# Two-layer encoder trunk on one core: the FFN's up product with the weights stationary and h born transposed

## Chip, cores and metric

One Trainium2 chip, one of its cores, one launch. The time is the device time of the whole program in microseconds (us). A kernel's time is the median of its runs.

## What is computed

`x` is (256 tokens, 1024). Each of two layers does FFN, mixer, FFN, each followed by a residual with a layer norm. The change touches the FFNs alone, which run four times:

```
def swiglu_ffn(x, w_up, w_down):          # w_up (1024, 2*2816), w_down (2816, 1024)
    gate, up = jnp.split(x @ w_up, 2, axis=-1)
    return (jax.nn.silu(gate) * up) @ w_down
x = layer_norm(ALPHA * x + 0.5 * swiglu_ffn(x, ffn1_w_up[l], ffn1_w_down[l]), ln1_g[l], ln1_b[l])
```

The mixer (a state-space branch and a sparse attention branch) stays as it is.

## The kernel before

**Products in three parts.** Every large product is made of fp32r matmuls on operands split in a high and a low part: `split_mm` issues hi·hi, hi·lo and lo·hi into the same PSUM bank (L617, L618, L619). ScalarE makes the high part of a weight slice (`whi`, L366, a copy of `raw`), VectorE the low part (`wlo`, L1009, `raw` minus `whi`). `x` is split in the same way (`xh`, `xl`).

**Weight slices.** SyncE loads slices of 128 x 1024 floats into `raw`, a ring of 4 buffers; `whi` and `wlo` are rings of 8. A slice may be split once TensorE has used the slice 8 places earlier, which the semaphore `pe_used` tells, and `raw` is loaded again when the slice in it is split (`split_done`).

**Up phase of an FFN.** The 2816 features go in 11 chunks of 256. A chunk has 4 weight slices; each holds two groups of 128 input rows, and for each 256 gate and 256 up columns. `up_pass` runs over a token tile t of 128 tokens: 8 x 3 matmuls, tokens stationary (128x128), 512 weight columns moving. A pass fills one bank: gate in one half, up in the other, tokens on partitions. Two passes make a chunk. Then ScalarE takes silu of the gate half (L387), VectorE multiplies it by the up half and 0.5 (L1035, `h`). `h_transpose` (L643) turns `h` of a chunk on TensorE, four transposes of 128x128, one chunk later; ScalarE copies the turned bank to `hh` (L378) and VectorE makes `hl` (L1025), because the down product needs features on partitions. The first two chunks are interleaved (`first_chunks`): pass 0 of both, then pass 1 of both, as the second token tile of `x` is ready later.

**Order.** Each engine has its own list, written out by hand. In chunk c, VectorE does: `h` of token tile 0, the four `wlo` of the slices of chunk c+2, `h` of tile 1, `hl` of chunk c-1. ScalarE has silu, four `whi`, silu, `hh`. The four `whi` wait for pass 1 of chunk c, which gives the slices free one by one.

**Down phase.** 22 slices, 12 matmuls of 512 columns each. In the first two FFNs ("first" and "second" in time) GpSimd (POOL) meanwhile prepares tables for the mixer of a layer (`prepare`): a long chain of elementwise operations on SBUF, begun early in the up phase. After the first down slice TensorE waits for its semaphore `bbar_ready` and turns its result (L723).

Of the kernel before, what the change touches and what calls it, by code (L numbers as in the profile page):

```python
# [68 lines left out]
OUT0 = BRS0 + BRANCH_Q  # L69
PEEL = 3  # L70
# [18 lines left out]
def build(nc, A, out):  # L89
# [10 lines left out]
    xh = sb("xh", [P, KT, SEQ], F32R)  # L100
    xl = sb("xl", [P, KT, SEQ], F32R)
# [40 lines left out]
    silu = place("silu", [P, NT, CW])  # L142
    h = place("h", [P, 2, NT, CW])
# [58 lines left out]
    for name in ("hi_done split_done pe_used ident_landed const_landed affine_landed const_ready tok_ready "  # L202
                 "xt_done xh_done x_ready up_done silu_done h_ready ht_done hh_done h_split acc_done "
# [9 lines left out]
    ACC = [2, 6]  # L213
    XT = [4, 6]
# [30 lines left out]

    def wait_up(eng, i, f, s, c, t):
# [18 lines left out]
    def xt_view(i):  # L265
        return ps[:, XT[i]:XT[i] + 2, :].rearrange("p b (k n) -> p (b k) n", n=P)
# [11 lines left out]
    with block:  # L278
# [80 lines left out]
        def _(act):  # L359
# [12 lines left out]
            def x_hi(t, i):  # L372
                act.wait_ge(S["xt_done"], 2 * t + i + 1)
                nc.scalar.copy(xh[:, :, tok(i)], xt_view(i)).then_inc(S["xh_done"], 1)  # L374

            def h_hi(f, c, b):
                act.wait_ge(S["ht_done"], steps(f, c) + 1)
                nc.scalar.copy(hh[:, bass.ds(2 * c, 2), :],  # L378
                               ps[:, 4 + b, :].rearrange("p (k n) -> p k n", k=2)).then_inc(S["hh_done"], 1)

            def up_chunk(i, f, s, c, b, first=False):
                for t in range(NT):
                    wait_up(act, i, f, s, c, t)
                    if not first:

                        act.wait_ge(S["h_ready"], 2 * steps(f, c) + t - 1)
                    nc.scalar.activation(silu[:, t, :], ps[:, 2 * b + t, 0:CW], ACT.Silu  # L387
                                         ).then_inc(S["silu_done"], 1)
# [3 lines left out]
                if not first:  # L392
                    h_hi(f, c - 1, 1 - b)
# [31 lines left out]
            def ffn(f, s0, prep):  # L425
                for c in range(PEEL):
                    up_chunk(0, f, s0 + 4 * c, c, c % 2, first=c == 0)
# [4 lines left out]
                    if c == 1 and prep is not None:  # L432
                        prepare_angles(prep)
                with act.Fori(0, LOOP_I) as i:
                    for e in range(2):
                        up_chunk(i, f, s0 + 4 * (PEEL + e), 2 * i + PEEL + e, (PEEL + e) % 2)
                for k in range(HK - RING):
                    splits(s0 + UP_Q + RING + k, 1)
                    if k == 5:
                        h_hi(f, NC_UP - 1, (NC_UP - 1) % 2)  # L440
# [84 lines left out]
            def mixer(l):  # L525
# [57 lines left out]
                def m_hi(t):  # L583
                    act.wait_ge(S["mt_done"], NT * l + t + 1)
                    src = xt_view(1) if t == 0 else ps[:, 0:2, :].rearrange("p b (k n) -> p (b k) n", n=P)
# [28 lines left out]
        def _(pe):  # L614
# [12 lines left out]
            def x_transpose(stage, i):  # L627
# [4 lines left out]
                for k in range(KT):  # L632
                    ins = nc.tensor.transpose(ps[:, XT[i] + k // 4, (k % 4) * P:(k % 4 + 1) * P],  # L633
# [3 lines left out]
            def h_transpose(f, c, b, reused=True):  # L637
                if reused:
                    pe.wait_ge(S["h_split"], steps(f, c) - 1)
                pe.wait_ge(S["h_ready"], 2 * steps(f, c) + 2)  # L640
                for k in range(2):
                    for i in range(NT):
                        ins = nc.tensor.transpose(ps[:, 4 + b, k * SEQ + i * P:k * SEQ + (i + 1) * P],  # L643
                                                  h[:, b, i, k * P:(k + 1) * P], ident[:, :])
                ins.then_inc(S["ht_done"], 1)

            def up_pass(i, f, s, c, b, t, wait_bank=True, between=None):

                if wait_bank:
                    pe.wait_ge(S["h_ready"], 2 * steps(f, c - 2) + t + 1)  # L650
                for q in range(4):
                    if t == 0:
                        wait_split(s + q, i)
                    for kk in range(2):
                        k = 2 * q + kk
                        a, b2 = kk * 512, kk * 512 + 512
                        ins = split_mm(ps[:, 2 * b + t, :], xh[:, k, tok(t)], xl[:, k, tok(t)],
# [8 lines left out]
            def up_chunk(i, f, s, c, b):  # L666
                for t in range(NT):
                    up_pass(i, f, s, c, b, t)

            def first_chunks(f, s, stage, prep):  # L670

                pe.wait_ge(S["x_ready"], 2 * stage + 1)
                up_pass(0, f, s, 0, 0, 0, False)
                up_pass(0, f, s + 4, 1, 1, 0, False, lambda: x_transpose(stage, 1))
                pe.wait_ge(S["x_ready"], 2 * stage + 2)
                up_pass(0, f, s, 0, 0, 1, False)
# [9 lines left out]
                up_pass(0, f, s + 4, 1, 1, 1, False)  # L686
                h_transpose(f, 0, 0, False)
# [9 lines left out]
            def late_pass(f, s, k0, n, ah, al, stage):  # L697


                for k in range(k0, n):  # L700
# [3 lines left out]
                    ins = wide_k(s + k, k, 0, ah, al, ACC[0], n - 1)  # L704
                ins.then_inc(S["acc_done"], 1)
                for k in range(k0, n):
                    ins = wide_k(s + k, k, 1, ah, al, ACC[1], n - 1)
# [31 lines left out]
            def ffn(f, stage, s0, following, prep):  # L739
                first_chunks(f, s0, stage, prep)  # L740
                for c in range(2, PEEL):
                    up_chunk(0, f, s0 + 4 * c, c, c % 2)
                    h_transpose(f, c - 1, (c - 1) % 2, False)
                with pe.Fori(0, LOOP_I) as i:
                    for e in range(2):
                        c = 2 * i + PEEL + e
                        up_chunk(i, f, s0 + 4 * (PEEL + e), c, (PEEL + e) % 2)
                        h_transpose(f, c - 1, (PEEL + e - 1) % 2)
                s = s0 + UP_Q
                for k in range(HK - RING):  # L750
# [3 lines left out]
                    for t in range(NT):  # L754
                        ins = wide_k(s + k, k, t, hh, hl, ACC[t], HK - 1)
                    ins.then_inc(S["pe_used"], 1)
                    if k == 5:
                        h_transpose(f, NC_UP - 1, (NC_UP - 1) % 2)
# [140 lines left out]
            def mixer(l):  # L899
# [59 lines left out]
                for k in range(OUT_Q):  # L959
                    wait_split(mix(l, OUT0 + k))  # L960
                    ins = wide_k(mix(l, OUT0 + k), k, 0, xh, xl, ACC[0], OUT_Q - 1)
# [5 lines left out]
                for k in range(OUT_Q):  # L967
                    ins = wide_k(mix(l, OUT0 + k), k, 1, xh, xl, ACC[1], OUT_Q - 1)
# [23 lines left out]
        def _(dve):  # L992
# [24 lines left out]
            def x_lo(stage, i):  # L1017
                dve.wait_ge(S["xh_done"], 2 * stage + i + 1)
                nc.vector.tensor_tensor(xl[:, :, tok(i)], xt_view(i), f32(xh[:, :, tok(i)]), ALU.subtract  # L1019
                                        ).then_inc(S["x_ready"], 1)  # L1020

            def h_lo(f, c, b):
                dve.wait_ge(S["hh_done"], steps(f, c) + 1)
                k = bass.ds(2 * c, 2)
                nc.vector.tensor_tensor(hl[:, k, :], ps[:, 4 + b, :].rearrange("p (k n) -> p k n", k=2),  # L1025
                                        f32(hh[:, k, :]), ALU.subtract).then_inc(S["h_split"], 1)

            def up_chunk(i, f, s, c, b, first=False, early=False):
                for t in range(NT):
                    dve.wait_ge(S["silu_done"], 2 * steps(f, c) + t + 1)  # L1030
                    if not early:

                        dve.wait_ge(S["ht_done"], steps(f, c) - 1)

                    nc.vector.scalar_tensor_tensor(out=h[:, b, t, :], in0=silu[:, t, :], scalar=0.5,  # L1035
                                                   in1=ps[:, 2 * b + t, CW:2 * CW], op0=ALU.mult,
                                                   op1=ALU.mult).then_inc(S["h_ready"], 1)
# [3 lines left out]
                if not first:  # L1041
                    h_lo(f, c - 1, 1 - b)

            def norm(n, s_end, i, aff):

                wait_acc(dve, n, s_end, i)
                for j in range(2):
                    cols = slice(512 * j, 512 * j + 512)
                    ins = nc.vector.scalar_tensor_tensor(out=x[:, i, cols], in0=x[:, i, cols], scalar=ALPHA,  # L1049
                                                         in1=ps[:, ACC[i] + j, :], op0=ALU.mult, op1=ALU.add)  # L1050
# [42 lines left out]
            def ffn(f, s0, prep):  # L1093
                for c in range(PEEL):
                    up_chunk(0, f, s0 + 4 * c, c, c % 2, first=c == 0, early=c < 2)
                    if c == 0 and prep is not None:
                        dve.wait_ge(S["par_t_ready"], 2 * prep + 1)
                        nc.vector.tensor_scalar(small[:, 0, :], par_t[:, 0:NJ], LAM_MAX, None, ALU.min
                                                ).then_inc(S["par_t_ready"], 1)
                with dve.Fori(0, LOOP_I) as i:  # L1100
                    for e in range(2):
                        up_chunk(i, f, s0 + 4 * (PEEL + e), 2 * i + PEEL + e, (PEEL + e) % 2)
# [496 lines left out]
```

## Time and profile before

| | |
|---|---|
| median of 3 runs | 1272.18 us (1271.83 to 1276.61) |
| the profiled execution | 1275.78 us, its span 1274.0 us |
| mean granted TensorE clock | 0.985 |
| busy: PE, VectorE (DVE), ScalarE (ACT), POOL | 1213.6, 781.9, 537.4, 405.2 us |

PE's busy time is modelled and overlapping (a 512-column matmul is shown with 0.39 us but the next starts after less), so how fast TensorE goes is read from start to start. Times in the timeline are us from the span's start.

### The profile page before, as it was taken

To read this page: it belongs to the slowest core of one execution; us is meant where nothing else is said; L and a number is where in the kernel's file an instruction comes from. 1 tells how busy PE (TensorE), PEld (TensorE's weight loads), DVE (VectorE), ACT (ScalarE), POOL (GpSimd) and SP (SyncE) were. 2 spreads that over 40 slices of the span, in tenths; PEclk is the share of its full clock that TensorE was granted. 3 is DMA by queue.
4 is the path that set the end of the run, shared out by engine and by line. 5 is a ranking of instruction groups with operands and counts; after the bars stand their busy time and mean duration, and the time that the engine had idled before them with its cause. 6 is when DMAs were issued, how large, how long until landed. Compare 5 with 4: busy or idle time off the path is not lost.

```text
span 1274.0 us, 17993 instructions
## 1 busy us (share of the span) xinstructions
PE 1213.6 (95%) x5952; PEld 980.3 (77%) x5952; DVE 781.9 (61%) x1278; ACT 537.4 (42%) x753; POOL 405.2 (32%) x599
## 2 busy tenths in 40 slices
PE   6999999989999989999999999989899999999997
PEld 5888777767677878887778888878677778788885
DVE  4657656567666775574376555375586668655543
ACT  5544432424435345443245444243344453544530
POOL 2889891141140068898600000002303300000000
PEclk9999999989999999999999999999899999999999
DMA  8757543542523575565447566445234345657640
GB/s 247 221 176 229 197 167 91 162 145 67 157 80 118 179 220 188 173 224 175 135 134 228 184 214 214 149 133 170 79 104 126 105 156 173 191 179 226 200 165 33
DMA packets 158289, 207.51 MB, mean 163 GB/s; under 512 B 13096, under 2 KB 107624, under 8 KB 158224
## 3 DMA queue, kind: packets, MB, share of 16 engines
q1 hardware_dynamic: 154352, 201.18, 49.5%
q10 hardware_dynamic: 2848, 3.89, 1.2%
q0 software_dynamic: 1024, 1.61, 0.6%
q8 instruction: 37, 0.61, 0.2%
q14 instruction: 28, 0.23, 0.1%
HBM read 205.56 MB, written 1.06 MB: 162 GB/s over the span
## 4 chain that ended last, share of the span: by engine, by line
PE 61%; POOL 23%; DVE 8%; issue 4%; ACT 2%; DMA 1%; POOLq 0%; SPq 0%; ACTq 0%; DVEq 0%
PE ps L617 17%; PE ps L619 16%; PE ps L618 16%; POOL small L1337 7%; POOL b_bar L1337 4%; DVE wlo L1009 3%; POOL tmp L1337 2%; POOL tab_s L1337 2%; POOL tab_c L1337 1%; POOL tab_s L1464 1%; PE ps L789 1%; PE ps L811 1%; PE ps L808 1%; PE ps L790 1%; PE ps L837 1%
## 5 line engine op out<-in xcount | busy, mean ns | idle before, releaser
L1009 DVE TENSOR_TENSOR wlo<-raw,whi 128x1024 fp32r<-128x1024 f32 (+1 forms) x372 | 474.3, 1292 | 241.2 <-ACT whi L366 227.5
L366 ACT CAST whi<-raw 128x1024 fp32r<-128x1024 f32 (+1 forms) x372 | 385.3, 1043 | 328.3 <-PE ps L619 289.3
L617 PE MATMUL ps<-whi,xh 128*128 128x512 f32 x1088 | 440.1, 405 | 12.4 <-DVE xl L1019 6.5
L619 PE MATMUL ps<-whi,xl 128*128 128x512 f32 x1088 | 426.3, 392 | 0.0
L618 PE MATMUL ps<-wlo,xh 128*128 128x512 f32 x1088 | 425.7, 391 | 0.0
L617 PEld LDWEIGHTS ps<-whi,xh 128*128 128x128 f32 x1088 | 207.3, 191 | 61.7 <-DVE xl L1019 7.4
L619 PEld LDWEIGHTS ps<-whi,xl 128*128 128x128 f32 x1088 | 206.8, 190 | 43.9
L618 PEld LDWEIGHTS ps<-wlo,xh 128*128 128x128 f32 x1088 | 207.7, 191 | 37.9
L1361 POOL TENSOR_TENSOR rstd<-var_eps,cst 128x1 f32<-128x1 f32 x12 | 18.2, 1517 | 555.2 <-DVE var_eps L1056 555.2
L617 PE MATMUL ps<-whi,hh 128*128 128x512 f32 x352 | 141.0, 401 | 0.0
L619 PE MATMUL ps<-whi,hl 128*128 128x512 f32 x352 | 138.7, 394 | 0.0
L618 PE MATMUL ps<-wlo,hh 128*128 128x512 f32 x352 | 137.9, 392 | 0.0
L1035 DVE SCALAR_TENSOR_TENSOR h<-silu,ps 128x256 f32<-128x256 f32 x88 | 36.5, 416 | 96.9 <-ACT silu L387 96.9
L387 ACT ACTIVATE silu<-ps 128x256 f32<-128x256 f32 x88 | 33.2, 379 | 139.0 <-PE ps L619 138.3
L1538 POOL TENSOR_TENSOR h_st<-tab_c,g_st 128x256 f32<-128x256 f32 x16 | 18.7, 1166 | 189.2 <-DVE g_st L1141 153.8
L619 PEld LDWEIGHTS ps<-whi,hl 128*128 128x128 f32 x352 | 66.5, 189 | 14.8
L618 PEld LDWEIGHTS ps<-wlo,hh 128*128 128x128 f32 x352 | 66.5, 189 | 13.9
L617 PEld LDWEIGHTS ps<-whi,hh 128*128 128x128 f32 x352 | 66.6, 189 | 13.3
L1337 POOL TENSOR_TENSOR small<-small 128x16 f32<-128x16 f32 x102 | 40.5, 397 | 8.5 <-ACT small L409 0.7
L1049 DVE SCALAR_TENSOR_TENSOR x<-x,ps 128x512 f32<-128x512 f32 x24 | 16.5, 686 | 43.1 <-PE ps L619 42.6
L374 ACT CAST xh<-ps 128x1024 fp32r<-128x1024 f32 x12 | 12.2, 1014 | 45.6 <-PE ps L633 45.6
L1025 DVE TENSOR_TENSOR hl<-ps,hh 128x512 f32 (+1 forms) x44 | 30.0, 683 | 0.0
(178 smaller groups left out, 1223.8 us busy)
## 6 DMA issues: line engine op xcount, KB each, us to landing
raw<-in_ffn_w_up SPq DMA_DIRECT2D x352, 256.0 KB, 4.0
raw<-in_ffn_w_down SPq DMA_DIRECT2D x176, 256.0 KB, 3.0
raw<-in_w_in SPq DMA_DIRECT2D x128, 256.0 KB, 3.2
raw<-in_w_branch SPq DMA_DIRECT2D x32, 256.0 KB, 2.8
raw<-in_w_out SPq DMA_DIRECT2D x32, 256.0 KB, 3.3
bias_g<-bias_rows ACTq DMA_DIRECT2D x16, 192.0 KB, 3.6
raw<-in_w_in SPq DMA_DIRECT2D x16, 148.0 KB, 2.3
affine<-in_ln_g SPq DMA_DIRECT2D x4, 512.0 KB, 5.5
```

Of the source, the lines that this page charges most:

```text
L366: nc.scalar.copy(whi[:, s % RING, 0:w], raw[:, s % RAW, 0:w]).then_inc(S["hi_done"], 1)
L387: nc.scalar.activation(silu[:, t, :], ps[:, 2 * b + t, 0:CW], ACT.Silu).then_inc(S["silu_done"], 1)
L617: nc.tensor.matmul(o, ah, bh, start=start, stop=False)
L618: nc.tensor.matmul(o, ah, bl, start=False, stop=False)
L619: return nc.tensor.matmul(o, al, bh, start=False, stop=stop)
L1009: nc.vector.tensor_tensor(wlo[:, s % RING, 0:w], raw[:, s % RAW, 0:w], f32(whi[:, s % RING, 0:w]), ALU.subtract).then_inc(S["split_done"], 1)
L1025: nc.vector.tensor_tensor(hl[:, k, :], ps[:, 4 + b, :].rearrange("p (k n) -> p k n", k=2), f32(hh[:, k, :]), ALU.subtract).then_inc(S["h_s ...
L1035: nc.vector.scalar_tensor_tensor(out=h[:, b, t, :], in0=silu[:, t, :], scalar=0.5, in1=ps[:, 2 * b + t, CW:2 * CW], op0=ALU.mult, op1=ALU. ...
L1049: ins = nc.vector.scalar_tensor_tensor(out=x[:, i, cols], in0=x[:, i, cols], scalar=ALPHA, in1=ps[:, ACC[i] + j, :], op0=ALU.mult, op1=ALU ...
L1337: ins = nc.gpsimd.tensor_tensor(o, a, b, f)
L1361: nc.gpsimd.tensor_tensor(rstd[:, i, :], var_eps[:, i, :], cst[:, 0:1], ALU.pow).then_inc(S["rstd_ready"], 1)
L1538: nc.gpsimd.tensor_tensor(h_re, co, g_re, ALU.mult)
```

## The change

The first two chunks of an FFN stay as they are (`tok_chunk`, tokens stationary). From chunk 2 on (`up_block`) a 128x128 block of weights is stationary and all 256 tokens move. For the 128 features t of a chunk, gate (g = 0) in bank 2t and up (g = 1) in bank 2t+1: `whi` meets `xh` and `xl` side by side, 512 moving columns, and `wlo` meets `xh`, 256 columns, added onto the first half. The bank then holds two halves that have yet to be added; VectorE does it for both banks with one `tensor_reduce` (`up_sum`). silu and the product run from SBUF to SBUF, `h` has its features on partitions, and its transposes are gone for these chunks. `hh` and `hl` are made from `h` in SBUF.

```diff
-            def up_chunk(i, f, s, c, b):
-                for t in range(NT):
-                    up_pass(i, f, s, c, b, t)
+            def up_block(i, f, s, c, t, after_tokens=False):
+                if after_tokens:
+                    pe.wait_ge(S["h_ready"], 2 * steps(f, t) + NT)
+                else:
+                    pe.wait_ge(S["sum_done"], sums(f, c - 1, t))
+                for g in range(2):
+                    both = ps[:, 2 * t + g, :].rearrange("p (v n) -> p v n", v=2)
+                    for q in range(4):
+                        if t == 0 and g == 0:
+                            wait_split(s + q, i)
+                        for kk in range(2):
+                            k = 2 * q + kk
+                            a = kk * 512 + g * CW + t * P
+                            nc.tensor.matmul(both, w(whi, s + q, a, a + P), xs[:, :, k, :], start=k == 0, stop=False)
+                            ins = nc.tensor.matmul(both[:, 0], w(wlo, s + q, a, a + P), xh[:, k, :], start=False,
+                                                   stop=k == KT - 1)
+                        if t == 1 and g == 1:
+                            ins.then_inc(S["pe_used"], 1)
+                    if after_tokens and t == 0 and g == 0:
+                        h_transpose(f, TOK_CHUNKS - 1)
+                if t == 0:
+                    ins.then_inc(S["up_done"], 1)
...
+            def up_chunk(i, f, s, c, tokens=False):          # VectorE
+                h_lo(f, c - 1, tokens)
+                for t in range(2):
+                    wait_up(dve, i, f, s, c, t)
+                    if not tokens:
+                        dve.wait_ge(S["h_ready"], 2 * steps(f, c - 1) + t + 1)
+                    nc.vector.tensor_reduce(up_sum[:, t, :, :],
+                                            ps[:, 2 * t:2 * t + 2, :].rearrange("p g (v n) -> p g n v", v=2),
+                                            mybir.AxisListType.X, ALU.add).then_inc(S["sum_done"], 1)
                     if t == 0:
+                        dve.wait_ge(S["h_split"], steps(f, c))
+                        for q in range(2):
                             split_lo(i, s + RING + q)
+                    dve.wait_ge(S["silu_done"], 2 * steps(f, c) + t + 1)
+                    nc.vector.scalar_tensor_tensor(out=h[:, t, :], in0=up_sum[:, t, 0, :], scalar=0.5,
+                                                   in1=up_sum[:, t, 1, :], op0=ALU.mult, op1=ALU.mult
+                                                   ).then_inc(S["h_ready"], 1)
+                    if t == 0:
+                        for q in range(2, 4):
+                            split_lo(i, s + RING + q)
...
-                    if k == 5:
-                        h_transpose(f, NC_UP - 1, (NC_UP - 1) % 2)
```

Two places of the order matter below. The first is TensorE at the start of chunk 2. Before, chunk 2 begins right behind the transposes of chunk 0, and those of chunk 1 follow only after all its 48 matmuls. The end of chunk 2 before (names: result <- moving, stationary):

```order
L617 MATMUL ps<-whi,xh 128x512
L618 MATMUL ps<-wlo,xh 128x512
L619 MATMUL ps<-whi,xl 128x512
L643 MATMUL ps<-ident,h 128x128 [waits h_ready]
L643 MATMUL ps<-ident,h 128x128 x3
```

Now, in the first quarter of chunk 2, behind its 16th matmul:

```order
L707 MATMUL ps<-xs,whi 128x512 [waits split_done]
L708 MATMUL ps<-xs,wlo 128x256
L707 MATMUL ps<-xs,whi 128x512
L708 MATMUL ps<-xs,wlo 128x256
L672 MATMUL ps<-ident,up_sum 128x128 [waits h_ready]
L672 MATMUL ps<-ident,up_sum 128x128 x3
L707 MATMUL ps<-xs,whi 128x512
L708 MATMUL ps<-xs,wlo 128x256
```

The transposes of chunk 1, with their wait for `h` of chunk 1, moved from the end of chunk 2 to its first quarter.

The second is VectorE in a chunk of the loop. Before:

```order
L1035 SCALAR_TENSOR_TENSOR h<-silu,ps 128x256 [waits ht_done,silu_done]
L1009 TENSOR_TENSOR wlo<-raw,whi 128x1024 [waits hi_done] x4
L1035 SCALAR_TENSOR_TENSOR h<-silu,ps 128x256 [waits ht_done,silu_done]
L1025 TENSOR_TENSOR hl<-ps,hh 128x512 [waits hh_done]
```

Now (the last chunk ahead of the loop, which has the loop's order):

```order
L1095 TENSOR_REDUCE up_sum<-ps 128x512 [waits up_done]
L1056 TENSOR_TENSOR wlo<-raw,whi 128x1024 [waits hi_done,h_split]
L1056 TENSOR_TENSOR wlo<-raw,whi 128x1024 [waits hi_done]
L1104 SCALAR_TENSOR_TENSOR h<-up_sum 128x256 [waits silu_done]
L1056 TENSOR_TENSOR wlo<-raw,whi 128x1024 [waits hi_done] x2
L1095 TENSOR_REDUCE up_sum<-ps 128x512 [waits pe_used]
L1104 SCALAR_TENSOR_TENSOR h<-up_sum 128x256 [waits silu_done]
```

The second reduction stands behind all four `wlo`, and it is what sets `sum_done` for TensorE's second block of the next chunk. `h` and, in the loop, `hl` read two tiles of SBUF instead of one and PSUM.

## Rows read from the trace of the kernel before

**Rows 1.** The page, part 1: busy us, share of the span, instructions.

```profile
PE 1213.6 (95%) x5952; PEld 980.3 (77%) x5952; DVE 781.9 (61%) x1278; ACT 537.4 (42%) x753; POOL 405.2 (32%) x599
```

**Rows 2.** Timeline of PE, one loop chunk of the third FFN: start, duration, engine, line.

```profile
697.21 0.48 PE L617 MATMUL ps<-whi,xh 128*128 128x512 f32 x1
...
702.78 0.39 PE L617 MATMUL ps<-whi,xh 128*128 128x512 f32 x1
...
708.23 0.60 PE L643 MATMUL ps<-ident,h 128*128 128x128 f32 x4
708.59 0.48 PE L617 MATMUL ps<-whi,xh 128*128 128x512 f32 x1
```

**Rows 3.** Timeline of PE, GLU of the mixer: first of 48 and what follows.

```profile
396.13 0.28 PE L617 MATMUL ps<-xh,whi 128*128 128x256 f32 x1
...
401.87 0.39 PE L617 MATMUL ps<-whi,ya_h 128*128 128x512 f32 x1
```

**Rows 4.** Timeline of PE: start of chunk 2 in FFNs two, three and four.

```profile
471.78 0.48 PE L617 MATMUL ps<-whi,xh 128*128 128x512 f32 x1
...
674.51 0.47 PE L617 MATMUL ps<-whi,xh 128*128 128x512 f32 x1
...
1101.17 0.48 PE L617 MATMUL ps<-whi,xh 128*128 128x512 f32 x1
```

**Rows 5.** Timelines of ACT and DVE: the end of chunk 1, same FFNs.

```profile
475.50 0.41 DVE L1035 SCALAR_TENSOR_TENSOR h<-silu,ps 128x256 f32<-128x256 f32 x1
...
676.93 1.05 ACT L366 CAST whi<-raw 128x1024 fp32r<-128x1024 f32 x1 [0.34 <-DMA raw<-in_ffn_w_up]
...
679.15 0.41 DVE L1035 SCALAR_TENSOR_TENSOR h<-silu,ps 128x256 f32<-128x256 f32 x1
...
1105.53 0.42 DVE L1035 SCALAR_TENSOR_TENSOR h<-silu,ps 128x256 f32<-128x256 f32 x1
```

**Rows 6.** Timelines of ACT and DVE in that loop chunk; four `wlo` back to back.

```profile
703.07 0.39 ACT L387 ACTIVATE silu<-ps 128x256 f32<-128x256 f32 x1 [4.20 <-PE ps L619]
704.34 1.05 ACT L366 CAST whi<-raw 128x1024 fp32r<-128x1024 f32 x1 [0.89 <-PE ps L619]
...
709.66 0.58 ACT L378 CAST hh<-ps 128x512 f32 x1
...
705.43 5.31 DVE L1009 TENSOR_TENSOR wlo<-raw,whi 128x1024 fp32r<-128x1024 f32 x4 [1.53 <-ACT whi L366]
710.66 0.42 DVE L1035 SCALAR_TENSOR_TENSOR h<-silu,ps 128x256 f32<-128x256 f32 x1
710.99 0.69 DVE L1025 TENSOR_TENSOR hl<-ps,hh 128x512 f32 x1
...
647.00 4.62 DVE L1009 TENSOR_TENSOR wlo<-raw,whi 128x1024 fp32r<-128x1024 f32 x4
```

**Rows 7.** Groups of DVE by shape: busy us, mean ns, idle before.

```profile
L1019 DVE TENSOR_TENSOR xl<-ps,xh 128x1024 fp32r<-128x1024 f32 x12 | 14.7, 1223 | 10.3 <-ACT xh L374 10.3
L1053 DVE BATCH_NORM_STATS2 stats<-x 128x6 f32<-128x512 f32 x24 | 16.7, 695 | 0.8
```

**Rows 8.** Timelines of POOL and DVE, late in the first two up phases.

```profile
101.72 1.05 POOL L1337 TENSOR_TENSOR b_bar<-tab_s,small 128x512 f32<-128x512 f32 x1
...
106.10 2.03 POOL L1337 TENSOR_TENSOR b_bar<-tab_s,small 128x512 f32<-128x512 f32 x1
...
103.96 7.48 DVE L1009 TENSOR_TENSOR wlo<-raw,whi 128x1024 fp32r<-128x1024 f32 x4 [1.42 <-ACT whi L366]
...
536.90 8.14 DVE L1009 TENSOR_TENSOR wlo<-raw,whi 128x1024 fp32r<-128x1024 f32 x4 [1.33 <-ACT whi L366]
```

**Rows 9.** Timeline of PE: its waits for POOL behind the first down slice.

```profile
145.28 0.44 PE L723 MATMUL ps<-ident,c_raw 128*128 128x128 f32 x2 [1.00 <-POOL b_bar L1337]
...
579.97 0.58 PE L723 MATMUL ps<-ident,c_raw 128*128 128x128 f32 x2 [2.76 <-POOL b_bar L1337]
```

**Rows 10.** Windows of PE: length, busy (instructions), granted clock, DMA share, GB/s.

```profile
580.20:583.40 3.20, 3.20 (x12) 0.50 0.67 223
```

More of the change, by code:

```diff
@@ L69 @@
 OUT0 = BRS0 + BRANCH_Q
+TOK_CHUNKS = 2
 PEEL = 3
@@ L141, in build @@
     hl = place("hl", [P, HK, SEQ], F32R)
-    silu = place("silu", [P, NT, CW])
-    h = place("h", [P, 2, NT, CW])
+    up_sum = place("up_sum", [P, 2, 2, CW])
+    h = place("h", [P, 2, CW])
     affine_at = at[0]
@@ L373, in x_hi, with h_hi, tok_chunk @@
                 act.wait_ge(S["xt_done"], 2 * t + i + 1)
[L374 to L381, printed above, removed]
+                nc.scalar.copy(xh[:, :, tok(i)], turned(xt_bank(t, i))).then_inc(S["xh_done"], 1)
+            def h_hi(f, c, tokens=False):
+                if tokens:
+                    act.wait_ge(S["ht_done"], TOK_CHUNKS * f + c + 1)
+                    src = ps[:, 4 + c, :].rearrange("p (k n) -> p k n", k=2)
+                else:
+                    act.wait_ge(S["h_ready"], 2 * steps(f, c) + 2)
+                    src = h[:, :, :]
+                nc.scalar.copy(hh[:, bass.ds(2 * c, 2), :], src).then_inc(S["hh_done"], 1)
+            def tok_chunk(f, s, c):
                 for t in range(NT):
[L383 to L384 removed]
+                    wait_up(act, 0, f, s, c, t)
+                    if c > 0:
                         act.wait_ge(S["h_ready"], 2 * steps(f, c) + t - 1)
[L387 removed]
+                    nc.scalar.activation(up_sum[:, t, 0, :], ps[:, 2 * c + t, 0:CW], ACT.Silu
+                                         ).then_inc(S["silu_done"], 1)
+                    if t == 0:
+                        for q in range(4):
+                            split_hi(0, s + RING + q)
+                if c > 0:
+                    h_hi(f, c - 1, True)
+            def up_chunk(i, f, s, c, tokens=False):
+                h_hi(f, c - 1, tokens)
+                for t in range(2):
+                    act.wait_ge(S["sum_done"], sums(f, c, t))
+                    nc.scalar.activation(up_sum[:, t, 0, :], up_sum[:, t, 0, :], ACT.Silu
                                          ).then_inc(S["silu_done"], 1)
@@ L425, in ffn @@
             def ffn(f, s0, prep):
-                for c in range(PEEL):
-                    up_chunk(0, f, s0 + 4 * c, c, c % 2, first=c == 0)
+                for c in range(TOK_CHUNKS):
+                    tok_chunk(f, s0 + 4 * c, c)
                     if c == 0 and prep is not None:
@@ L740, in ffn @@
                 first_chunks(f, s0, stage, prep)
-                for c in range(2, PEEL):
-                    up_chunk(0, f, s0 + 4 * c, c, c % 2)
-                    h_transpose(f, c - 1, (c - 1) % 2, False)
+                for c in range(TOK_CHUNKS, PEEL):
+                    up_chunk(0, f, s0 + 4 * c, c, c == TOK_CHUNKS)
                 with pe.Fori(0, LOOP_I) as i:
@@ L1093, in ffn @@
             def ffn(f, s0, prep):
-                for c in range(PEEL):
-                    up_chunk(0, f, s0 + 4 * c, c, c % 2, first=c == 0, early=c < 2)
+                for c in range(TOK_CHUNKS):
+                    tok_chunk(f, s0 + 4 * c, c)
                     if c == 0 and prep is not None:
```

116 lines of the change are left out of this document (64 added, 52 removed).

## The prediction

> **What bounds the kernel now.** The page first: PE is busy for 95% of the span, VectorE for 61% [rows 1]. PE's busy time is modelled, so I read its pace from starts. In a chunk of the third FFN the second pass has 24 matmuls from 702.78 to the transposes at 708.23, 0.227 us each, and nothing waits; chunk to chunk it is 708.59 - 697.21 = 11.38 [rows 2]. 48 x 0.227 is 10.90, so the four transposes cost 0.48 with the restart behind them. TensorE's own issue is therefore the bound of the up phase. Two places differ. In the first two FFNs PE stands behind the first down slice until POOL's chain delivers, 1.00 and 2.76 us [rows 9]. And late in the same two up phases POOL and VectorE hold each other up: a POOL operation that takes 1.05 when VectorE is quiet takes 2.03, and four `wlo` that take 4.62 alone (5.31 where `whi` paces them) take 7.48 and 8.14 [rows 6, 8].
>
> **TensorE's work.** No 128x128 load with 256 moving columns is in the up phase before, but the GLU has 48 of them: (401.87 - 396.13) / 48 = 0.120 us each [rows 3]. A chunk becomes 32 pairs of 0.227 + 0.120, that is 11.09 us in place of 10.90: the same columns, but 64 matmuls instead of 48. Against that stand the transposes, 0.48. For 36 chunks and 36 sets of transposes (chunk 10's lay in the down phase): 36 x (0.19 - 0.48) = -10.4 us. I take it in full; [rows 3] is the same shape.
>
> The row shows a load of 128 columns and 256 moving columns in 0.120 us, so the load hides behind the matmul ahead of it. The Trainium skill speaks against the change here ("TensorE: Matmul & The Clock Gate", The mechanism): weight loads overlap matmuls only when their row group differs. Its figure for a load, columns / 1.2, would make 107 ns for each of 16 more loads, an estimate of +62 us over 36 chunks. The trace disagrees, since 107 for the load and 107 for the columns don't fit into 120 ns.
>
> **The moved transposes.** Chunk 1's `h` is now wanted 16 matmuls (2.8 us) into chunk 2. When is it there? Chunk 2 starts at 471.78, 674.51 and 1101.17 in FFNs two to four [rows 4], so it is wanted at 474.6, 677.3 and 1104.0. VectorE's second `h` of chunk 1 ends at 475.9, 679.6 and 1105.95 [rows 5]: it is queued behind four `wlo`, those behind `whi`, and the last `whi` waited for a load until 676.93 [rows 5]. None of this changes. PE stalls for 1.3, 2.3 and 2.0: +5.6 us. (In the first FFN `h` is about in time; I take zero.)
>
> **VectorE's added work and the new rounds.** A reduction of 1024 PSUM elements is nowhere in the trace. Nearest above it in kind is BN_STATS, 0.695 for 512 inputs, twice that 1.39; nearest in size a 1024-element operation from PSUM, 1.22; below, one with 512 outputs, 0.69 [rows 6, 7]. I take 1.22, as it reads 1024, and 0.68 and 1.39 as bounds. Back to back VectorE's operations start sooner than they end: `wlo` every 1.14 (4.62 for four), `h` 0.33 ahead of the next [rows 6].
>
> Two rounds must fit into 11.09. One goes through TensorE: the second block of a chunk may start only when the reduction behind the four `wlo` of the chunk before is done. From the start of such a block: 8 pairs and 2 more, 3.47, free the first slice (before, the slices came free over a whole pass, now over the last quarter of a chunk); 0.20 later `whi` starts (704.34 against 702.78 + 6 x 0.227); 1.05 `whi`; 0.04; four `wlo` 4.56; `h` 0.33; reduction 1.22; 0.04 back: 10.9. The other is VectorE and ScalarE alone: reduction to silu, `h`, `hh` (0.58), `hl`, reduction, silu, `whi`, four `wlo`, `h`, again 10.9 [rows 6]. Both fit with 0.2 to spare, so where POOL is quiet the third and fourth FFN keep 11.09.
>
> **Where POOL is busy.** With a `wlo` every 2.0 instead of 1.14 (8.14 / 4) and up to 1.0 of wait for the two-tile `h`, the first round is 3.47 + 1.29 + 8.1 + 1.3 + 1.26 = 15.4: PE idles over 4 us in such a chunk. Before, the same contention cost PE nothing: VectorE needed 8.14 + 2 x 0.33 + 0.69 = 9.5 of 11.38 us, and PE waited for none of it before two chunks later. I laid the lists of both FFNs out, in order, with these durations: the last three chunks take 12.6, 16.0, 12.5 in the first FFN and 15.3, 15.9, 12.4 in the second, instead of 11.1; with 0.3 in each elsewhere this is +8.2 and +10.4: +18.6 us.
>
> The rows show only that `wlo` (both inputs in SBUF) and POOL take turns, and that `h` from PSUM is 0.42 as ever. The Trainium skill has the rule ("SBUF — State Buffer", Who interferes with whom): an operation with two SBUF inputs contends with POOL, one with at most one does not, and a reduction never does. By it the new `h` and `hl` join the fight and the reduction stays out, as the sum has it; were they free too, it would be some 3 us less.
>
> **What is given back.** PE arrives late at the first down slice, so its waits for POOL vanish: -3.8 [rows 9]. Behind the second one the granted clock was 0.50 (1.2 GHz) for 3.2 us of work [rows 10], half of which is lost; without that wait -1.6. But PE now idles for over 4 us about four times, longer than the 2.76 that this drop followed, and 2.3 us once; where the clock falls, 1.6 each. I take three such: +4.5 or so.
>
> Sum: -10.4 + 5.6 + 18.6 - 3.8 - 1.6 + 4.5 = +12.9 us. The profiled execution took 1275.78 (span 1274.0) and would take 1288.7; it stood 3.6 above the median of 1272.18, so the median becomes 1285.
>
> **Rivals.**
> (A) *The reduction is short or VectorE slips past POOL.* At 0.68 the last chunks add 9 instead of 18.6 and the clock drops are fewer: 1272.2 + 12.9 - 9.6 - 3 = 1272.5. For it: only 512 results. Against it: in [rows 7] the time follows the inputs. 0.18.
> (B) *VectorE's round binds in every chunk.* 0.2 is thin; the loop's register instructions ahead of each wait, or a reduction of 1.39 (strided by a half bank), would put the period at 11.3 to 11.5. Decides from 11.4 on, where the whole saving per chunk is gone: + 36 x 0.3 = +11, 1296, at worst 1300. 0.17.
> (C) *The gain arrives.* The moved transposes find `h` in time, or their wait costs nothing, and the contended chunks hide: what is left is -10.4, less what POOL's chain takes back in the first two FFNs (their 18 chunks end at POOL's time anyway): -5 to -8, about 1265. It decides if the reduction is so short that the round stays under 11.1 with `wlo` at 2.0, for which it would have to be below nothing (3.47 + 1.29 + 8.1 alone is 12.9). 0.06.
> (D) *The load doesn't hide when matmuls of 512 and 256 columns alternate.* A load is shown with 0.165 us on average (980.3 / 5952, [rows 1]); 0.045 more than 0.12 for 32 pairs in 36 chunks is +52 us: 1325. [rows 3] speaks against it: 0.04.
> My forecast: 0.55.
>
> **The numbers.** The range runs from (A) to the worst of (B): 1270 to 1300, and leaves out D, most of C and some of the tails, 0.17. A measurement here tells about 0.5% (6.4 us) from no change. Slower by more: D, B, and of my forecast all but 0.07, and little of A: 0.70. Within: most of A, the low end of mine, some of C: 0.23. Faster: the rest of C and what I haven't thought of, 0.07.
>
> **What would show it.** Start to start 0.227 and 0.120 in turn in a chunk, period 11.09 in FFNs three and four. In FFNs two to four an idle of 1.3 to 2.3 us on PE in the first quarter of chunk 2, released by VectorE's `h`. In the last three chunks of the first two FFNs PE idle for 4 us ahead of the second block, released by the reduction. The waits of [rows 9] gone. The prediction is wrong if the reduction is far from 1.22, if chunks 8 to 10 keep 11.1 beside POOL, or if alternating matmuls pace differently.

## The result and the profile after

The changed kernel takes **1317.47 us** (median of 4, 1309.8 to 1319.17), the kernel before, run beside it, 1273.15 us: ratio 1.033, 95% interval 1.029 to 1.038. The forecast was 1285 with a range to 1300. The sign was right, the size was not: +44 us instead of +13. The profiled execution took 1318.29 us; its span is 42.4 us longer than that of before.

The page, part 1, against [rows 1], and parts of its groups (part 5):

```profile
span 1316.4 us, 18957 instructions
PE 1225.8 (93%) x6384; PEld 1003.7 (76%) x6384; DVE 860.2 (65%) x1350; ACT 534.8 (41%) x753; POOL 393.6 (30%) x599
...
L1095 DVE TENSOR_REDUCE up_sum<-ps 128x512 f32<-128x1024 f32 x72 | 87.6, 1217 | 3.6 <-PE ps L708 3.6
```

The reduction takes 1.217 us, as I had taken (1.22). PE is busy for 12 us more and a smaller share of the span, so TensorE waits more. The waits of PE (total us, number, longest):

```profile
PE ps L707 <- DVE up_sum L1095: 17.4, 8, 4.4
PE ps L664 <- DVE x L1130: 10.1, 5, 2.5
PE ps L672 <- DVE up_sum L1079: 6.9, 4, 2.2
PE ps L851 <- POOL h_st L1406: 6.9, 2, 3.5
PE ps L774 <- issue: 6.7, 2, 3.4
```

Three are new. L707 is the start of a block, which waits for a reduction. L672 is the transposes of chunk 1. L774 is the first thing behind the first down slice, where [rows 9] had 1.00 and 2.76 us. (The same line waits for POOL's later results as well: 4.5 us in six waits, where the kernel before had 2.8 in four.)

**Start to start.** From one chunk's start to the next, read from the starts of PE's blocks in the trace, us:

| chunk | 2 | 3 | 4 | 5 | 6 | 7 | 8 | 9 | 10 | 2 to 10 |
|---|---|---|---|---|---|---|---|---|---|---|
| FFN one | 12.57 | 11.19 | 11.38 | 11.60 | 12.08 | 17.69 | 17.59 | 12.07 | 11.31 | 117.5 |
| FFN two | 15.68 | 11.23 | 11.44 | 11.36 | 15.34 | 12.88 | 17.50 | 12.02 | 11.31 | 118.8 |
| FFN three | 13.91 | 11.14 | 11.31 | 11.30 | 11.31 | 11.31 | 11.30 | 11.31 | 11.31 | 104.2 |
| FFN four | 13.89 | 11.15 | 11.22 | 11.32 | 11.31 | 11.31 | 11.30 | 11.31 | 11.31 | 104.1 |

Before, the same stretch took 102.3 to 102.4 in each FFN. So 35 of the 42 us lie in these stretches, 31 of them in the first two FFNs. And there is a surprise in the quiet FFNs: 11.31 where I had 11.09.

**Beside POOL.** Timelines, first FFN, chunks 7 and 8 (PE, then DVE):

```profile
106.81 0.80 PE L707 MATMUL ps<-xs,whi 128*128 128x512 f32 x1 [3.58 <-DVE up_sum L1095]
...
124.83 0.80 PE L707 MATMUL ps<-xs,whi 128*128 128x512 f32 x1 [3.80 <-DVE up_sum L1095]
...
100.13 1.50 DVE L1104 SCALAR_TENSOR_TENSOR h<-up_sum 128x256 f32<-128x256 f32 x1
101.56 4.06 DVE L1056 TENSOR_TENSOR wlo<-raw,whi 128x1024 fp32r<-128x1024 f32 x2
105.54 1.21 DVE L1095 TENSOR_REDUCE up_sum<-ps 128x512 f32<-128x1024 f32 x1
```

The second block of the chunk waits until the reduction at 105.54 is done, and that stands behind two `wlo` of 2.0 us (1.2 when POOL is quiet) and an `h` of 1.50 (0.42 when POOL is quiet). The reduction itself is as fast as ever. Windows of PE over these chunks and over quiet ones (length, busy, granted clock, DMA share, GB/s):

```profile
105.90:112.70 6.80, 5.89 (x18) 0.50 0.38 120
122.97:129.80 6.83, 4.97 (x15) 0.50 0.87 253
726.30:737.40 11.10, 11.10 (x66) 1.00 0.61 189
748.70:760.00 11.30, 11.30 (x66) 1.00 0.61 186
```

Around the end of each of these two waits the granted clock is 0.50, that is 1.2 GHz, for 6.8 us; for 0.9 and 1.9 us of that PE still stands idle. In the second FFN it is 0.50 for 3.4 us at each of the two longest waits (2.6 and 4.4 us), and stays at full around the third (1.4 us).

**The first down slice.** The timeline of PE, then of DVE, in the first FFN:

```profile
158.71 0.40 PE L650 MATMUL ps<-whi,hl 128*128 128x512 f32 x1
162.46 0.41 PE L774 MATMUL ps<-ident,c_raw 128*128 128x128 f32 x2 [3.35 <-issue]
...
157.96 2.35 DVE L1056 TENSOR_TENSOR wlo<-raw,whi 128x1024 fp32r<-128x1024 f32 x2
160.23 1.21 DVE L1095 TENSOR_REDUCE up_sum<-ps 128x512 f32<-128x1024 f32 x1
161.93 0.42 DVE L1104 SCALAR_TENSOR_TENSOR h<-up_sum 128x256 f32<-128x256 f32 x1 [0.48 <-ACT up_sum L418]
```

"issue" means that the view names no releaser. PE resumes just after the last `h` of chunk 10 (161.93 + 0.42 = 162.35): the transposes for POOL's tables have a second wait, for that `h` (it keeps them out of banks that chunk 10 still uses). Before, that `h` was long done; now it is the last thing of VectorE's chunk, behind the last `wlo`, the reduction and silu.

### The profile page after: what moved, and what is told of

Read it like the earlier page. It is cut to its first block, busy times and chain, and to the rows that moved or that the text cites. A ratio compares the mean times of both kernels' runs of the same rounds, so it can differ in the third digit from the quotient of the medians.

```text
span 1316.4 us, 18957 instructions
## 1 busy us (share of the span) xinstructions
PE 1225.8 (93%) x6384; PEld 1003.7 (76%) x6384; DVE 860.2 (65%) x1350; ACT 534.8 (41%) x753; POOL 393.6 (30%) x599
## 4 chain that ended last, share of the span: by engine, by line
PE 64%; DVE 15%; POOL 7%; issue 6%; ACT 4%; DMA 3%; SPq 0%; DVEq 0%; ACTq 0%; POOLq 0%
PE ps L707 14%; PE ps L648 12%; PE ps L650 11%; PE ps L649 11%; DVE wlo L1056 7%; PE ps L708 7%; DMA raw<-in_ffn_w_up 2%; ACT whi L381 2%; DVE up_sum L1095 2%; PE ps L836 1%; POOL b_bar L1406 1%; POOL tmp L1406 1%; PE ps L858 1%; PE ps L855 1%; PE ps L884 1%
## 5 line engine op out<-in xcount | busy, mean ns | idle before, releaser
L707 PE MATMUL ps<-xs,whi 128*128 128x512 f32 x1152 | 416.5, 405 | 17.5 <-DVE up_sum L1095 17.4
L708 PE MATMUL ps<-xs,wlo 128*128 128x256 f32 x1152 | 326.3, 283 | 0.0
L707 PEld LDWEIGHTS ps<-xs,whi 128*128 128x128 f32 x1152 | 220.8, 192 | 74.8 <-DVE up_sum L1095 21.9
L648 PE MATMUL ps<-whi,xs 128*128 128x512 f32 (+1 forms) x512 | 213.6, 417 | 12.3 <-DVE xs L1066 6.3
L708 PEld LDWEIGHTS ps<-xs,wlo 128*128 128x128 f32 x1152 | 221.9, 193 | 0.0
L649 PE MATMUL ps<-wlo,xs 128*128 128x512 f32 (+1 forms) x512 | 202.2, 395 | 0.0
L650 PE MATMUL ps<-whi,xs 128*128 128x512 f32 (+1 forms) x512 | 202.1, 395 | 0.0
L648 PEld LDWEIGHTS ps<-whi,xs 128*128 128x128 f32 x512 | 100.0, 195 | 40.4 <-DVE xs L1066 7.2
L418 ACT ACTIVATE up_sum<-up_sum 128x256 f32<-128x256 f32 x72 | 30.1, 418 | 217.2 <-DVE up_sum L1095 217.2
L650 PEld LDWEIGHTS ps<-whi,xs 128*128 128x128 f32 x512 | 99.4, 194 | 21.1
L649 PEld LDWEIGHTS ps<-wlo,xs 128*128 128x128 f32 x512 | 100.2, 196 | 16.6
L1095 DVE TENSOR_REDUCE up_sum<-ps 128x512 f32<-128x1024 f32 x72 | 87.6, 1217 | 3.6 <-PE ps L708 3.6
L648 PEld LDWEIGHTS ps<-whi,hh 128*128 128x128 f32 x352 | 66.5, 189 | 14.2
```

What stands on the lines that cost most here:

```text
L418: nc.scalar.activation(up_sum[:, t, 0, :], up_sum[:, t, 0, :], ACT.Silu).then_inc(S["silu_done"], 1)
L648: nc.tensor.matmul(o, ah, bh, start=start, stop=False)
L649: nc.tensor.matmul(o, ah, bl, start=False, stop=False)
L650: return nc.tensor.matmul(o, al, bh, start=False, stop=stop)
L707: nc.tensor.matmul(both, w(whi, s + q, a, a + P), xs[:, :, k, :], start=k == 0, stop=False)
L708: ins = nc.tensor.matmul(both[:, 0], w(wlo, s + q, a, a + P), xh[:, k, :], start=False, stop=k == KT - 1)
```

## The experiments

All ran beside the kernel before; ratios are to it. Times of one kernel scatter with the granted clock: some 50 runs of the kernel before lie between 1271.25 and 1282.24 us, with a mean granted clock of 0.991 down to 0.982. So a part of a gain that shows as less time at 0.50 in one profile need not belong to the edit.

**1. Are the interleaved operands slow to read?** In `xs` the 256 high and the 256 low columns of a group lie 2048 elements apart; here the 512 moving columns are contiguous.

```diff
-xs = sb("xs", [P, 2, KT, SEQ], F32R)
+xs = sb("xs", [P, KT, 2, SEQ], F32R)
```

> The changed kernel with xs laid out as [P, KT, 2, SEQ], so that the 512 moving columns of a hi/lo pair lie side by side instead of in two runs of 256. In the changed kernel a pair (512 + 256 columns) takes 0.3535 us where 0.347 was forecast. Theory A (the two runs cost): pairs at 0.347, loop chunks of the third and fourth FFN at 11.1 instead of 11.31, about -8 us in all. Theory B (the cost comes with the alternation of 512 and 256 columns, or with 64 loads in place of 48): pairs stay at 0.3535, chunks at 11.31, no change in time.

Measured: 1308.78 (1307.54 to 1316.92), ratio 1.029 (1.024 to 1.033), which overlaps that of the changed kernel. The quiet chunks stay at 11.31. The layout is not the cause. (The profiled span is 9.7 us shorter all the same, as much as Theory A asked for, but the chunks of the four FFNs give only 0.4 of it; the clock was at 0.50 for 44.4 us instead of 64.8, the last 10 us left out here and below.)

**2. The wait at the first down slice.** The transposes wait for the reduction of chunk 10's first block (which frees their banks) in place of the last `h`.

```diff
-pe.wait_ge(S["h_ready"], 2 * steps(f, NC_UP - 1) + NT)
+pe.wait_ge(S["sum_done"], sums(f, NC_UP - 1, 0))
```

> The changed kernel; the first transposes for the mixer's tables (prep_transpose, q = 0) wait for the first reduction of chunk 10, which is the last reader of banks 0 and 1, instead of for the last h. Theory A (this wait, queued behind four wlo, a reduction, silu and a product, is what holds PE 3.35 and 3.38 us at the first down slice in the first two FFNs): both idles vanish, -6.7 us, and -1.6 more where the granted clock no longer falls behind the second one: -7 to -8.5. Theory B (POOL's b_bar, named as releaser in the kernel before, still ends last): the idles stay, 0.

Measured: 1301.83 (1299.21 to 1305.18), ratio 1.021 (1.017 to 1.025). The wait at L774 for the last `h` is gone; 2.1 us came back twice, one step on (L785). The gain, 15.6 us, is twice what I expected, though the waits at L774 and L785 together are only 4.3 us shorter; the clock was at 0.50 for 34.1 us instead of 64.8, of which half, some 15 us, is lost time (an estimate). Whether the edit or chance spared those drops isn't shown. The other waits stay:

```profile
PE ps L707 <- DVE up_sum L1095: 18.7, 8, 4.9
...
PE ps L672 <- DVE up_sum L1079: 7.4, 4, 2.4
```

**3. The place of the reduction in VectorE's list.** Same operations, another order: reduction 0, `h` 0, one `wlo`, reduction 1, three `wlo`, `h` 1 (the new calls alone are shown).

```diff
+total(0)
+product(0)
+split_lo(i, s + RING)
+total(1)
+for q in range(1, 4):
+    split_lo(i, s + RING + q)
+product(1)
```

> The changed kernel with VectorE's list in a chunk reordered: reduction 0, h 0, wlo 0, reduction 1, wlo 1 to 3, h 1 (was: reduction 0, wlo 0 and 1, h 0, wlo 2 and 3, reduction 1, h 1). Nothing else moves. Theory A (PE's idles of 2.6 to 4.4 us late in the first two up phases come from the round through the second reduction, which stands behind four wlo): the round has over 3 us to spare, no idle over 2.5 us there and no fall of the granted clock behind one; the long chunks (17.7, 17.6; 15.3, 17.5) come to 13.4 to 13.8, which is VectorE's own throughput beside POOL; -18 to -25 us in all. Theory B (VectorE beside POOL has too little throughput in any order): the long chunks stay at 15 or more, less than -6 us.

Measured: 1287.79 (1286.88 to 1289.14), ratio 1.011 (1.007 to 1.014): 30 us less than the changed kernel with nothing but an order changed, and more than the 18 to 25 I expected, as the long chunks came down to 12.6 and below and not to 13.4 or more. Windows over two chunks of the third FFN, and the waits of PE, of which the first grew, since the last `h` is now later still:

```profile
713.00:724.10 11.10, 11.10 (x67) 1.00 0.63 194
757.00:768.10 11.10, 11.10 (x67) 1.00 0.60 185
```

```profile
PE ps L774 <- issue: 9.9, 2, 5.1
...
PE ps L672 <- DVE up_sum L1079: 7.3, 4, 2.7
```

Chunks 3 to 8 take 11.09 in all four FFNs, beside POOL too; chunk 9 takes 12.5 in the first two. So POOL's turn-taking costs TensorE little if the reduction doesn't stand behind all four `wlo`, and the 11.31 of the quiet chunks is no property of the matmuls.

**4. POOL out of the way.** The tables' doubling steps work on 2 columns instead of up to 64 (two lines of the edit are shown).

```diff
-c0, s0 = tab_c[:, js, 0:n], tab_s[:, js, 0:n]
-c1, s1 = tab_c[:, js, n:2 * n], tab_s[:, js, n:2 * n]
+c0, s0 = tab_c[:, js, 0:m_], tab_s[:, js, 0:m_]         # m_ = min(n, 2)
+c1, s1 = tab_c[:, js, n:n + m_], tab_s[:, js, n:n + m_]
```

> The changed kernel with POOL's table doublings cut to 2 columns per step (the tables are zeroed at the start; this part of the computation is left out, and the mixer works on wrong tables of the same size). Theory A (the long chunks are VectorE and POOL taking turns on operations of 256 and 512 columns): chunks 3 to 10 of the first two FFNs take 11.31 as in the third and fourth, no low clock in these up phases, -20 to -26 us. Theory B (the long chunks come from something in the order of the first two FFNs that POOL has no part in): they stay.

Measured: 1290.71 (1288.08 to 1293.27), ratio 1.013 (1.009 to 1.017). The chunks of 15 to 18 us are gone (all from 3 on are 11.2 to 11.5, but chunk 8 of the first two FFNs with 12.3). The waits for the last `h` stay, the quiet chunks stay at 11.31.

**5. The transposes of chunk 1 later.**

```diff
-if after_tokens and t == 0 and g == 0:
+if after_tokens and t == 0 and g == 1:
```

> The changed kernel with one edit: the transposes of chunk 1's h stand after the second group of eight pairs of chunk 2 (32 matmuls in) instead of after the first. My account: h of chunk 1 comes 4.8 to 5.0 us after the start of chunk 2 in FFNs two to four and the transposes would now be reached after 5.55, so the idles of 2.23, 2.02 and 2.01 us ahead of them and the 0.69 of the first FFN go, and with the longest of them perhaps the low clock behind it (1.7): 7 to 9 us less than the changed kernel, 1309 to 1311. Rival (the round of VectorE moves out with the later hh and hl, and the idle comes back as a wait for the reduction in chunk 3): no gain, 1316 to 1319, and chunks 3 in the profile longer than 11.3.

Measured: 1298.94 (1296.83 to 1302.79), ratio 1.018 (1.015 to 1.020). The wait at L672 is gone from PE's waits, chunk 2 takes 11.6 to 11.8 instead of 12.6 to 15.7. The gain, 18 us, is twice what I expected. Of 20.7 in the spans 11.9 lie in the four stretches from chunk 2 to the down phase, 6.9 of them the stall itself. Of the other 8.8, 7.7 lie between the up phases of the third and the fourth FFN, where the code is the same and the clock was at 0.50 for 3.4 us instead of 20.5 (41 us in all against 64.8). The rival is seen once: in the second FFN chunk 3 takes 12.38.

**6 and 7. Early reductions with the earlier wait, and with the later transposes as well.**

> The changed kernel with two edits together: VectorE's list with each reduction as early as it can be (as e3_redearly) and the first down slice's transposes waiting for the reduction of chunk 10's first block instead of its last h (as e2_sumwait). In the run with the early reductions alone PE stood 5.06 and 4.84 us ahead of those transposes in the first two FFNs, since VectorE's last h is now behind all of its list. My account: both idles go, 10 less, perhaps 1.7 for each low clock behind them: 1275 to 1279 against the 1287.8 of the early reductions alone. Rival (the idle is really POOL's chain, as it was before the change): the idle moves to the next POOL wait with 1.0 to 2.8 us in each of the two FFNs and little more than half is gained, 1281 to 1284.

Measured: 1282.76 (1278.78 to 1286.28), ratio 1.005 (1.003 to 1.007): 5 us less than the early reductions alone, not 10, which is in the rival's range, though not for its reason. A part of the wait came back one step on, at the next thing behind the transposes, which waits for a VectorE copy of their result (the same in run 2, 2.1 us in each of the two FFNs). And the second FFN ran at the slower pace, with 13.4, 14.2 and 12.7 for chunks 7 to 9 where run 3 had 11.1, 11.1 and 12.6. The timeline of PE, first FFN:

```profile
151.46 0.28 PE L785 MATMUL ps<-c_t,b_bar 128*32 128x32 f32 x7 [2.98 <-DVE c_t L1151]
```

> e6_redwait and e5_htlate together. If the costs are separate: the sum of both gains, 7 to 9 less than e6_redwait, 1267 to 1272, which would be level with the kernel before or 0.3% better. The remaining gain of TensorE's pace (11.09 for a chunk instead of 11.38, 33 or so chunks, 9.6 us) would then be offset by the chunks beside POOL that are still 12.5 and by the low clock. Rival (the later transposes delay the next reduction, or PE meets the low clock elsewhere): 1275 to 1280.

Measured: 1276.17 (1274.01 to 1279.68), ratio 1.000 (0.998 to 1.002). 6.6 less than experiment 6: level with the kernel before, and not better. That is the rival's time, not the sum of both gains (1267 to 1272). The pace differs by FFN: the third ran its chunks from 3 on at 11.09, the fourth at 11.31, the first two at 11.3 until POOL's longer operations, though in all of them the reductions are early.

**8. The control: POOL cut in the kernel before.** The same edit as in 4.

> A control: the kernel BEFORE with POOL's tables of the first two FFNs cut to two columns for each doubling step, the same cut as e4_poolshort (part of the computation is left out: most of the cosine and sine tables stay zero). It shows what POOL's work costs without the change. My account from the profile before: only the waits for POOL of 1.0 and 2.8 us and the low clock behind the second (1.6) go: 4 to 6 us less, 1267 to 1269. Then of the 26.8 us that the same cut gave the changed kernel 21 to 23 are the change's own. Rival (POOL's work slows the kernel before as well, by clock or by VectorE): 10 us or more less, 1262 or below, and the change is less to blame for what stands beside POOL.

Measured: 1269.48 (1263.93 to 1274.41), ratio 0.994 (0.992 to 0.997). So POOL costs the kernel before 0.6%, 7 us (4 to 10 by the interval, so my 4 to 6 is not excluded), and the changed kernel 2.0% (1.033 - 1.013), 26 us.

**9. What sets TensorE's pace.** One transpose that nobody reads, at the start of each chunk from 3 on, in the kernel of 7.

```diff
+if t == 0:
+    nc.tensor.transpose(ps[:, 6, 0:P], ident[:, :], ident[:, :])
 pe.wait_ge(S["sum_done"], sums(f, c - 1, t))
```

> e7_redwaitht with one idle-work transpose (128x128 of the identity into a bank that nobody reads then) on TensorE at the start of every chunk from 3 on. In the traces so far a pair of matmuls takes 0.3465 us or 0.3535 us, which makes a chunk of 11.09 or of 11.31; one or the other is kept for whole phases, and it changes only at a break in TensorE's row (a wait of even 0.1 us, or transposes). The kernel before had transposes in every chunk and always came back to its faster pace (0.2267) behind them. Theory (a transpose puts the row back on the faster pace): every chunk of all four FFNs is 11.09 + 0.12 to 0.25, that is 11.2 to 11.35, no phase at a steady 0.3535; time 1273 to 1278. Rival (the pace behind a break is a matter of chance or of the wait): some chunks at 0.3465 and others at 0.3535 in each FFN, a chunk 11.3 to 11.5 on average, 1278 to 1284. Neither would be much better than e7_redwaitht; the run is for the cause.

Measured: 1272.76 (1271.13 to 1280.42), ratio 0.998 (0.996 to 1.000), the fastest whole version with the change, though its interval overlaps that of run 7. Windows over two chunks of the third FFN (the first is one of the three slow ones), and the timeline of PE at the break between them:

```profile
702.20:713.61 11.41, 11.41 (x67) 1.00 0.60 185
713.61:724.82 11.21, 11.21 (x67) 1.00 0.60 187
```

```profile
713.61 0.27 PE L699 MATMUL ps<-ident 128*128 128x128 f32 x1
713.64 0.47 PE L709 MATMUL ps<-xs,whi 128*128 128x512 f32 x1
713.95 0.28 PE L710 MATMUL ps<-xs,wlo 128*128 128x256 f32 x1
714.07 0.40 PE L709 MATMUL ps<-xs,whi 128*128 128x512 f32 x1
```

Of the 32 chunks that begin so, 29 run at 0.347 to 0.348 us for a pair and three at 0.353, each for one chunk only; without it whole FFNs stayed at 0.3535. Against a chunk at the slower pace (11.31) the one with an operation that computes nothing is 0.1 us shorter, against one at the faster pace (11.09) 0.12 longer. The four stretches add up to 413.9 us in both profiles, this one and that of run 7, so in all nothing was gained in them; the run is for the cause. The clock was at 0.50 for 13.6 us here and 20.5 in run 7.

**10. POOL cut in the kernel of 7.**

> e7_redwaitht with POOL's tables cut to two columns for each doubling step, as in c8_before_poolshort (part of the computation is left out: most of the cosine and sine tables stay zero). With POOL out of the way in both, it shows against c8_before_poolshort what the stationary-weight form is worth by itself. Theory (TensorE's own saving arrives when nothing else stands in its way): 33 to 36 chunks at 11.09 to 11.31 instead of 11.38, that is 2 to 10 us less than c8_before_poolshort (1269.5, ratio 0.9943): 1260 to 1267, ratio 0.986 to 0.993. Rival (VectorE's round still costs, or first slices and low clock take it back): no better than c8_before_poolshort, ratio 0.994 or more.

Measured: 1268.44 (1263.45 to 1272.0), ratio 0.992 (0.990 to 0.995). Against the control's 0.994 (0.992 to 0.997) that is unresolved. The profile is clearer: in all four FFNs chunk 2 takes 11.82 and the others 11.31, nothing waits in them, and the stretch is 102.3, the very number of the kernel before (102.3 in the control). This execution ran wholly at the slower pace, with the reductions early and no wait that could have set it: chunk 2 began at it, behind the transposes of chunk 0, in all four FFNs.

## Why the prediction was wrong

**The parts of the sum.** Measured ones are of the changed kernel's profile against that of before, us; the low clock counts half of what the clock rows at 0.50 cover outside the last 10 us (64.8 against 34.1).

| term | forecast | measured |
|---|---|---|
| TensorE's work, 36 chunks | -10.4 | -2.5 (36 x (11.31 - 11.38)) |
| waits of the moved transposes | +5.6 | +6.9 |
| chunks beside POOL (6 to 10 of FFNs one and two) | +18.6 | +16.5 (26.7 over 11.31, less 10.2 by the clock) |
| first waits behind the first down slice | -3.8 | +3.0 (6.7 instead of 3.8) |
| low clock | +2.9 | +15.3 |
| sum | +12.9 | +39.2 |

The rest of the 42.4 is 3.2: 1.8 for the later waits at L774 (4.5 instead of 2.8), short waits in the chunks ahead of the long ones, and what I can't place. Half of the time at 0.50 is an upper bound of what it cost, as PE stood idle for 4.5 us of it (3.2 before). The term is not one execution's: the mean granted clock was 0.973 to 0.981 in the four runs of the changed kernel and 0.982 to 0.991 in those of the kernel before.

**Beside POOL: right in kind and in size.** The idle is where it was said to be, ahead of the second block, released by the reduction, 1.4 to 4.4 us in the five long cases and 0.5 to 0.6 in three more. The chunks were off (6 to 8, not 8 to 10). Runs 4 and 8 give the size independently: the cut of POOL is worth 26 us to the changed kernel and 7 to the one before, 18 us net, where my terms that hang on POOL add to 17.7 (18.6 - 3.8 - 1.6 + 4.5). That the totals meet so closely is in part luck: the idles in the chunks came to 16.5 instead of 18.6, and the low clock in them to up to 10.2 instead of 4.5. By the Trainium skill ("SBUF — State Buffer", Who interferes with whom) a reduction never contends and an operation with two SBUF inputs does; the trace agrees (reduction 1.21 beside POOL, 1.22 alone; `h` 1.50 against 0.42).

**The failed part is the quiet one.** With POOL cut in both kernels, the change costs 24.4 us by the spans (1286.5 - 1262.1), where my sum without the POOL terms is -4.8. Of the 24.4, 11.9 lie in the four stretches (8.4 of it waits), 8.4 in the waits at L774 (11.2 instead of 2.8), and the other 4 elsewhere; in all the clock was at 0.50 for 37.5 us instead of 13.7. Three steps failed.

*"Two rounds must fit into 11.09 ... Both fit with 0.2 to spare."* They don't. Timelines of ACT and DVE, third FFN, one round of VectorE and ScalarE:

```profile
735.42 0.42 ACT L418 ACTIVATE up_sum<-up_sum 128x256 f32<-128x256 f32 x1 [2.04 <-DVE up_sum L1095]
735.75 3.88 ACT L381 CAST whi<-raw 128x1024 fp32r<-128x1024 f32 x4
...
734.17 1.22 DVE L1095 TENSOR_REDUCE up_sum<-ps 128x512 f32<-128x1024 f32 x1
736.82 2.36 DVE L1056 TENSOR_TENSOR wlo<-raw,whi 128x1024 fp32r<-128x1024 f32 x2 [1.43 <-ACT whi L381]
739.10 0.42 DVE L1104 SCALAR_TENSOR_TENSOR h<-up_sum 128x256 f32<-128x256 f32 x1
739.43 2.35 DVE L1056 TENSOR_TENSOR wlo<-raw,whi 128x1024 fp32r<-128x1024 f32 x2
741.70 1.22 DVE L1095 TENSOR_REDUCE up_sum<-ps 128x512 f32<-128x1024 f32 x1
743.40 0.42 DVE L1104 SCALAR_TENSOR_TENSOR h<-up_sum 128x256 f32<-128x256 f32 x1 [0.48 <-ACT up_sum L418]
744.78 0.69 DVE L1073 TENSOR_TENSOR hl<-h,hh 128x512 f32 x1 [0.95 <-ACT hh L398]
745.39 1.22 DVE L1095 TENSOR_REDUCE up_sum<-ps 128x512 f32<-128x1024 f32 x1
```

Reduction to reduction is 745.39 - 734.17 = 11.22: 2.65 to the first `wlo` (reduction, silu, `whi` in turn), 4.88 for `wlo`, `h`, `wlo`, 1.70 to the next `h`, 1.38 through `hh` to `hl`, 0.61. With 11.22 against 11.09 TensorE must wait, and it does, by a hair. The timeline of PE at the second block of chunk 4, where the reduction of 741.70 has just ended (742.92):

```profile
742.61 0.40 PE L707 MATMUL ps<-xs,whi 128*128 128x512 f32 x1
742.85 0.28 PE L708 MATMUL ps<-xs,wlo 128*128 128x256 f32 x1
742.98 0.50 PE L707 MATMUL ps<-xs,whi 128*128 128x512 f32 x1
743.31 0.28 PE L708 MATMUL ps<-xs,wlo 128*128 128x256 f32 x1
```

This is rival (B)'s mechanism, but (B) priced it at the round's own length. What follows is larger: in this FFN the pairs took 0.3465 until there, and from there to its end 0.3535, 32 x 0.3535 = 11.31. That is longer than the round, so nothing waits any more, and the waits view shows nothing. With the reductions early (run 3) that wait is not met and the 11.09 holds to chunk 8 or further. But the wait is not the only way to the slower pace: in runs 7 and 10, reductions early too, seven of eight FFNs ran at it from chunk 2 on, behind transposes. With a transpose in each chunk (run 9) chunk 2 is slow in all four FFNs and chunk 3 fast in all four. The kernel before had transposes in every chunk; its [rows 2] show 0.227, while its down phases, without them, run at 0.229. So the four transposes that I booked as 0.48 us saved may have done something for the pace as well; no run takes them alone out of the kernel before. At 11.31 the stationary form is worth 0.07 a chunk, and one stretch is as long as before.

*"PE arrives late at the first down slice, so its waits for POOL vanish: -3.8."* POOL was early, but the transposes have another wait, for the last `h` of chunk 10, which the change delays, and that became the one that ends last. Runs 2 and 6 show it, for a part of the time: with that wait moved, 4.3 and 3.7 us came back at L785. I had read who released PE before and not what else the instruction waits for.

*"I take three such: +4.5 or so."* The clock was at 0.50 for 30.7 us more, not 6. The four longest waits for the reduction had 20.5 of it, two of them 6.8 each, twice what [rows 10] show for one. The stall ahead of chunk 1's transposes in the second FFN had 3.4. The wait at the first down slice there kept its own 3.4, which I had booked as given back. And the mixers, whose code didn't change, had 13.7 and 17.1 instead of 10.2 and 13.7. The versions without the new waits have less (13.6 us in run 9 against 64.8 in the changed kernel and 34.1 before).

**What was right.** The alternating pair, 0.227 + 0.120 at the faster pace (rival D is out, whose 1325 is 1272 and 52 and leaves out the +12.9; and with it the Trainium skill's rule on weight loads, as the prediction cites it: the load of 128 columns hides here), the reduction at 1.22 (A is out), the stalls of 2.23, 2.02 and 2.01 ahead of the moved transposes (1.3, 2.3 and 2.0 forecast), and the sign.

**Open.** Which of the two paces TensorE takes behind a break. Of the 19 blocks from chunk 3 on that began late in the changed kernel (first pair over 0.38 us) 10 led to the slower one and 9 to the faster; in run 7 it was 3 of 4 behind a wait. Behind the transposes in chunk 2 of run 7 it was 7 of 8, behind the single ones of run 9 only 3 of 32, and in the kernel before none. And why the clock is lower for longer in mixers whose code is the same, which is most of what run 5 gained beyond the forecast.

## What to carry to other kernels

A margin of 0.2 us in a round of 16 operations on two engines, added up, is no margin: ask what order the list could have that makes it 2 us, as moving the reduction ahead of three `wlo` did for 30 us. When a result is made later than before, look up every wait on its semaphore, in the next phase too, and at instructions that another wait bounds now. And if an engine is suspected of a conflict, cut its work in both kernels: the difference of the two cuts is the change's share.

## What the hardware showed

TensorE has two steady paces at full granted clock for the same instructions: 0.3465 and 0.3535 us for a 512- and a 256-column matmul, 0.2267 and 0.2289 for a 512-column one. It keeps one, with a single exception found (the second half of a down phase of the kernel before, near 647.4), until its row is broken by a wait or by transposes, and the break may lead to either. A useless transpose per chunk (0.12 us) brought 29 of 32 chunks to the faster pace and was just repaid by it. And a pause of about 0.1 us of TensorE was followed by 0.2 us more in each chunk to the end of the third FFN's up phase.
